# Which of the six weight transfers of an odd expert go to the two spare places

## The reference, cut to what matters

```python
def expert_block(args):
    xb, e = args
    return (jax.nn.silu(xb @ w_gate[e]) * (xb @ w_up[e])) @ w_down[e]
```

```python
def expert_block(args):
    xe, e = args
    gu = xe @ w_gu[e] + b_gu[e]
    x_glu = jnp.minimum(gu[:, :D_FF], SWIGLU_LIMIT)
    x_lin = jnp.clip(gu[:, D_FF:], -SWIGLU_LIMIT, SWIGLU_LIMIT)
    act = (x_lin + 1) * (x_glu * jax.nn.sigmoid(SWIGLU_ALPHA * x_glu))
    return act @ w_dn[e] + b_dn[e]
```

## Time and profile before

| | us |
|---|---|
| median of 3 runs | 1977.25 |
| lowest, highest | 1975.54, 1978.81 |
| profiled execution | 1975.73 |
| its span, first to last instruction | 1973.9 |

### The profile page before, as it was taken

One profiled execution on the slowest core, in us unless ns is written; L12 is line 12 of the kernel. 1 busy time (PEld: TensorE's weight loads), 2 busy tenths in 40 slices (PEclk: granted clock), 3 DMA queues, 4 the chain that ended last, 5 costly groups with the idle time before them and its releaser, 6 DMA issues.

```text
span 1973.9 us, 27226 instructions
## 1 busy us (share of the span) xinstructions
PE 1793.9 (91%) x10815; PEld 988.7 (50%) x10816; DVE 522.7 (26%) x1208; ACT 394.9 (20%) x912; POOL 51.0 (3%) x109
## 2 busy tenths in 40 slices
PE   7999999986867999899999999998897999989987
PEld 4766777754544667678743333333333333333332
DVE  4685331132212240342541111111111111111112
ACT  3343552021101220433111110011110111101111
POOL 0040000000000010100010000000000000000000
PEclk9999999998978999999999999999999999999999
DMA  9979315439999752423466999999999799999996
GB/s 398 409 268 394 138 65 216 168 150 394 422 411 413 303 109 93 84 59 102 167 261 257 428 427 428 427 429 427 429 427 428 292 427 428 428 428 428 427 428 284
DMA packets 57691, 626.81 MB, mean 318 GB/s; under 512 B 7360, under 2 KB 11456, under 8 KB 13472
## 3 DMA queue, kind: packets, MB, share of 16 engines
q1 hardware_dynamic: 55744, 620.09, 76.2%
q0 software_dynamic: 1584, 4.33, 2.1%
q10 hardware_dynamic: 272, 1.05, 0.1%
HBM read 624.39 MB, written 1.05 MB: 317 GB/s over the span
## 4 chain that ended last, share of the span: by engine, by line
PE 59%; DMA 32%; DVE 3%; issue 3%; ACT 2%; DVEq 0%; SPq 0%; ACTq 0%
PE ps L500 57%; DMA ring<-in_w_gu_dram 27%; DMA ring<-in_moe_w_gate_dram 4%; PE ps L667 2%; DMA ring<-in_w_dn_dram 1%; ACT arena L1549 1%; ACT arena L1720 1%; DMA hN<-in_x_dram 1%; DVE stat L2114 0%; DVE arena L2131 0%; SPq L525 0%; PE ps L663 0%; DVEq L1992 0%; DVE hN L2007 0%; DVE rstd L1963 0%
## 5 line engine op out<-in xcount | busy, mean ns | idle before, releaser
L500 PE MATMUL ps<-ring,arena 128*64 128x512 f32 (+2 forms) x4416 | 734.9, 553 | 97.7 <-DMA ring<-in_w_gu_dram 48.5
L500 PEld LDWEIGHTS ps<-ring,arena 128*64 128x64 f32 (+1 forms) x4416 | 242.6, 128 | 534.6 <-issue 418.0
L500 PE MATMUL ps<-arena 128*32 128x256 f32 (+13 forms) x2434 | 382.6, 452 | 38.3 <-ACT arena L1549 15.5
L500 PEld LDWEIGHTS ps<-arena 128*64 128x64 f32 (+8 forms) x2434 | 171.2, 146 | 225.3 <-issue 157.7
L500 PE MATMUL ps<-hT,ring 128*128 128x256 f32 (+1 forms) x960 | 236.1, 401 | 5.0 <-DVE hT L2040 2.0
L500 PEld LDWEIGHTS ps<-hT,ring 128*128 128x128 f32 x960 | 179.4, 191 | 60.5 <-issue 35.6
L1549 ACT ACTIVATE arena<-ps 128x512 f32<-128x512 f32 (+4 forms) x191 | 104.7, 571 | 312.2 <-PE ps L500 178.2
L2385 DVE TENSOR_SCALAR arena<-ps 128x512 f32<-128x512 f32 (+1 forms) x34 | 23.0, 676 | 509.5 <-PE ps L500 509.5
L1815 ACT ACTIVATE arena<-ps,mod,gain 128x128 f32<-128x128 f32 x176 | 66.1, 458 | 422.4 <-PE ps L500 422.4
L1827 ACT ACTIVATE arena<-arena 128x512 f32<-128x512 f32 (+1 forms) x44 | 25.3, 575 | 567.4 <-DVE arena L2385 375.9
L500 PEld LDWEIGHTS ps<-arena,hN 128*128 128x128 f32 x896 | 104.6, 193 | 32.4 <-issue 18.0
(11 more groups left out here) (306 smaller groups left out, 908.3 us busy)
## 6 DMA issues: line engine op xcount, KB each, us to landing
ring<-in_w_gu_dram SPq DMA_DIRECT2D x96, 2048.0 KB, 25.5
ring<-in_w_dn_dram SPq DMA_DIRECT2D x64, 2048.0 KB, 21.4
arena<-in_w_gu_dram SPq DMA_DIRECT2D x32, 2048.0 KB, 27.3
ring<-dense_dram SPq DMA_DIRECT2D x56, 1024.0 KB, 8.9
ring<-in_moe_w_up_dram SPq DMA_DIRECT2D x16, 2048.0 KB, 15.7
ring<-in_moe_w_down_dram SPq DMA_DIRECT2D x16, 2048.0 KB, 15.0
ring<-in_ada_w_dram SPq DMA_DIRECT2D x24, 1024.0 KB, 18.0
ring<-in_w_mod_dram SPq DMA_DIRECT2D x24, 1024.0 KB, 7.8
```

Source lines behind the costliest of these rows:

```text
L500: ins = nc.tensor.matmul(*a, start=start, stop=stop, **k)
```

## The change

The spare places now hold d = 4 and d = 5 of every odd unit, in both mixtures. Places, transfers, sizes and products stay as they are. What moves is which chunks of which unit wait for which reader: d = 0 to 3 always wait for the unit just ahead, and d = 4, 5 for the one before that. Ahead of the loops the two spare places are still filled right behind unit 0, now with d = 4, 5 of unit 1.

```diff
+ALONE = CHUNKS - SPARES
...
             def moe1_spare(group, d):
-                sp.dma_start(spare[d], moe1_source(group, d)).then_inc(spare_full[1][d], 16)
+                sp.dma_start(spare[d - ALONE], moe1_source(group, d)).then_inc(spare_full[1][d - ALONE], 16)
...
-            for d in range(SPARES):
+            for d in range(ALONE, CHUNKS):
                 moe1_spare(1, d)
-            for d in range(SPARES, CHUNKS):
+            for d in range(ALONE):
                 free1(d, 1)
                 moe1_chunk(1, d)
             with sp.Fori(1, E // 8) as it:
                 for d in range(CHUNKS):
-                    free1(d, it * 2 - 1 if d < SPARES else it * 2)
+                    free1(d, it * 2 if d < ALONE else it * 2 - 1)
                     moe1_chunk(it * 2, d)
-                for d in range(SPARES):
-                    sp.wait_ge(gates_used, it * 2)
-                    moe1_spare(it * 2 + 1, d)
-                for d in range(SPARES, CHUNKS):
+                for d in range(ALONE):
                     free1(d, it * 2 + 1)
                     moe1_chunk(it * 2 + 1, d)
+                for d in range(ALONE, CHUNKS):
+                    free1(d, it * 2)
+                    moe1_spare(it * 2 + 1, d)
...
-                    free1(d, E // 4 - 1 if d < SPARES else E // 4)
+                    free1(d, E // 4 if d < ALONE else E // 4 - 1)
...
                 for d in range(CHUNKS):
-                    free2(d, it * 2 - 1 if d < SPARES else it * 2)
+                    free2(d, it * 2 if d < ALONE else it * 2 - 1)
                     moe2_chunk(it * 2, d)
-                for d in range(SPARES):
+                for d in range(ALONE):
+                    free2(d, it * 2 + 1)
+                    moe2_chunk(it * 2 + 1, d)
+                for d in range(ALONE, CHUNKS):
                     free2(d, it * 2)
                     moe2_spare(it * 2 + 1, d)
-                for d in range(SPARES, CHUNKS):
-                    free2(d, it * 2 + 1)
-                    moe2_chunk(it * 2 + 1, d)
...
-                if u == 1 and d < SPARES:
-                    pe.wait_ge(spare_full[1][d], it * 16 + 16)
-                    w = spare[d]
+                if u == 1 and d >= ALONE:
+                    pe.wait_ge(spare_full[1][d - ALONE], it * 16 + 16)
+                    w = spare[d - ALONE]
                 else:
-                    pe.wait_ge(part_full[1][d], it * 16 + 16 if d < SPARES else it * 32 + 16 * u + 16)
+                    pe.wait_ge(part_full[1][d], it * 32 + 16 * u + 16 if d < ALONE else it * 16 + 16)
                     w = chunk_ap(moe1_at, d)
```

More of the change, by code:

```diff
@@ L573, in moe2_spare @@
             def moe2_spare(e, d):
-                sp.dma_start(spare[d], moe2_source(e, d)).then_inc(spare_full[2][d], 16)
+                sp.dma_start(spare[d - ALONE], moe2_source(e, d)).then_inc(spare_full[2][d - ALONE], 16)
             def free2(d, experts):
@@ L1220, in rows2 @@
                 d, part = j // CHUNK, j % CHUNK
-                if u == 1 and d < SPARES:
+                if u == 1 and d >= ALONE:
                     if part == 0:
-                        pe.wait_ge(spare_full[2][d], it * 16 + 16)
-                    w = spare[d]
+                        pe.wait_ge(spare_full[2][d - ALONE], it * 16 + 16)
+                    w = spare[d - ALONE]
                 else:
                     if part == 0:
-                        pe.wait_ge(part_full[2][d], it * 16 + 16 if d < SPARES else it * 32 + 16 * u + 16)
+                        pe.wait_ge(part_full[2][d], it * 32 + 16 * u + 16 if d < ALONE else it * 16 + 16)
                     w = chunk_ap(moe2_at, d)
```

## The result

The changed kernel takes 1985.09 us in the median of 20 executions (1978.87 to 1996.04), the kernel before 1978.86 us in 20 executions on the same chip (1973.43 to 1984.66). The ratio is 1.0038, with a 95% interval of 1.0027 to 1.0049: slower by 5 to 10 us. (The ratio is worked out from all executions and is not the quotient of the two medians, which would be 1.0031.) The forecast of 1979.8 us was wrong, and the time lies just above its range. The profiled execution of the changed kernel took 1983.8 us, its span 1982.0 us.

The account below looks back on a forecast made before the run. It took the first mixture as bound by TensorE's sequencer and the second by the stream of transfers. Costs of 1.8 + 0 + 0.3 + 0.5 = 2.6 us on 1977.25 gave 1979.8 us, range 1975.2 to 1984.

Follow-up runs that it names:

- hold_up: The changed kernel with one more wait: SyncE issues group 1's up chunks only after group 0's down products; 1988.84 us, ratio 1.0055 to the kernel before.
- down_first: The changed kernel, but inside the first mixture's loop SyncE sends an odd group's down chunks ahead of its gate and up chunks; 1994.62 us, ratio 1.0074 to before.
- hole_last: The kernel before with one extra wait, at group 7 alone: its gate chunks wait for group 6's gate products; 1982.62 us, ratio 1.0021.

## What to carry to other kernels

Where a loader waits for a consumer, count from that release to the last arrival behind it and from the same release to its need, and compare the two. A shift of both is no cover, and a difference under a microsecond or two is a coin toss that deserves a large chance. When two bounds lie within 3% of each other, as 58.8 us of transfer and 60.5 us of TensorE for two groups do here, a version that only trades loading ahead at one end of a unit for the other has little to win: the change, hold_up and down_first each moved a wait to another chunk. down_first was slower than the change itself by 3.8 thousandths, hold_up by 1.7, which its interval does not resolve.

## What was new about the hardware

A jump of TensorE to code that must be fetched took 2.85 us beside 169 GB/s of transfers, 3.45 beside 280 and 5.0 to 6.4 beside full traffic (425 GB/s in the changed kernel). Where TensorE waited 1.66 to 1.95 us for a transfer instead of its usual 0.80 us, the products behind ran at a granted clock of 0.51 to 0.58, and the 32 of them took 1.6 to 1.7 us longer: more than the 0.9 to 1.15 us that the wait itself added. A stream of 2 MiB transfers that restarts from empty lands its first after 8.1 us in hole_last; in down_first, where two chunks were still in flight, it is 14.2.
